# Expert step of a mixture-of-experts layer: rows turned behind the gather, down weights laid as 8 KB runs

## The reference

```python
gu = xb @ w_up[e] + b_up[e]                  # (rows, 1024) x (1024, 2048)
gate, up = gu[:, :D_EXPERT], gu[:, D_EXPERT:]
gate = jnp.minimum(gate, SWIGLU_LIMIT)
up = jnp.clip(up, -SWIGLU_LIMIT, SWIGLU_LIMIT)
act = (up + 1.0) * (gate * jax.nn.sigmoid(SWIGLU_ALPHA * gate))
return act @ w_down[e] + b_down[e]           # (rows, 1024) x (1024, 1024)
```

## Time and profile before

| | before |
|---|---|
| median of three runs | 1363.99 us |
| the profiled execution's own time | 1364.04 us |
| its span, first to last instruction | 1362.3 us |
| PE busy / DVE / ACT / POOL | 1196.0 / 584.2 / 255.3 / 494.5 us |
| DMA packets, bytes | 110953, 448.96 MB |
| HBM read | 447.00 MB |

### The profile page before, as it was taken

The page is one execution under the profiler, slowest core; times in us unless marked ns, Lnnn a source line. Parts: engine busy times, 40 slices in busy tenths (PEclk is TensorE's granted clock), DMA queues, the critical chain, the costliest instruction groups (busy, mean ns, idle before and its releaser), DMA issues.

```text
span 1362.3 us, 30127 instructions
## 1 busy us (share of the span) xinstructions
PE 1196.0 (88%) x11131; PEld 585.9 (43%) x11132; DVE 584.2 (43%) x1229; ACT 255.3 (19%) x497; POOL 494.5 (36%) x813
## 2 busy tenths in 40 slices
PE   5899999999999997797699779869799798699996
PEld 3677777775543343232233223323234233233333
DVE  0699971211353443433244424424244344244444
ACT  3001122200122221221122112111122121122222
POOL 0183120000141344455444544544445445444330
PEclk9898999999799999998899889989899899899998
DMA  8963333345489599999999999999999999999981
GB/s 255 317 196 108 111 119 124 99 153 220 174 358 382 197 397 418 418 418 417 419 417 416 416 419 418 418 418 418 416 416 417 417 418 414 418 418 409 398 345 59
DMA packets 110953, 448.96 MB, mean 330 GB/s; under 512 B 8526, under 2 KB 42894, under 8 KB 78107
## 3 DMA queue, kind: packets, MB, share of 16 engines
q1 hardware_dynamic: 110190, 446.57, 83.0%
q10 hardware_dynamic: 685, 1.17, 0.3%
q0 software_dynamic: 48, 0.85, 0.2%
HBM read 447.00 MB, written 2.42 MB: 330 GB/s over the span
## 4 chain that ended last, share of the span: by engine, by line
PE 60%; DMA 11%; POOL 8%; issue 8%; DVE 7%; SPq 5%; ACT 0%; DVEq 0%; POOLq 0%
PE banks L1290 21%; PE banks L1093 12%; PE banks L1300 12%; DMA ring<-in_w_down 10%; POOL ring L508 6%; DVE R L762 4%; PE banks L1021 3%; SPq L383 3%; PE banks L1075 3%; PE banks L1054 2%; PE banks L1205 2%; POOL big L477 1%; PE banks L1061 1%; POOL prod L499 1%; PE banks L1084 1%
## 5 line engine op out<-in xcount | busy, mean ns | idle before, releaser
L1290 PE MATMUL banks<-ring,hT 128*32 128x512 f32 x3328 | 441.5, 625 | 99.1 <-POOL ring L508 84.2
L508 POOL COPY ring<-big 128x512 f32<-128x512 f32 x248 | 142.2, 621 | 567.9 <-SPq L389 567.9
L508 POOL COPY ring<-R 128x512 f32<-128x512 f32 x496 | 287.1, 623 | 133.4 <-DMA R<-in_w_up 131.2
L309 DVE TENSOR_TENSOR xt<-xt,banks 128x1024 f32<-128x1024 f32 x106 | 128.8, 1215 | 432.6 <-PE banks L1075 432.6
L1300 PE MATMUL banks<-ring,hT 128*32 128x256 f32 x3328 | 229.8, 396 | 11.5 <-DMA ring<-in_w_down 10.0
L1093 PE MATMUL banks<-hT,ring 128*128 128x288 f32 x768 | 195.6, 417 | 7.9 <-ACT stage L535 6.0
L1290 PEld LDWEIGHTS banks<-ring,hT 128*32 128x32 f32 x3328 | 98.7, 113 | 236.2 <-POOL ring L508 106.5
L1300 PEld LDWEIGHTS banks<-ring,hT 128*32 128x32 f32 x3328 | 110.5, 115 | 196.9 <-issue 129.4
L1093 PEld LDWEIGHTS banks<-hT,ring 128*128 128x128 f32 x768 | 149.3, 196 | 50.6 <-ACT stage L535 6.4
L654 ACT COPY WT<-banks 128x256 f32<-128x256 f32 x52 | 19.4, 372 | 537.9 <-PE banks L1300 537.9
L762 DVE SCALAR_TENSOR_TENSOR R<-big,convw,R 128x256 f32<-128x256 f32 x240 | 99.7, 490 | 0.0
(11 more groups left out here) (225 smaller groups left out, 770.3 us busy)
## 6 DMA issues: line engine op xcount, KB each, us to landing
ring<-in_w_down SPq DMA_DIRECT2D x128, 1024.0 KB, 11.7
R<-in_w_up SPq DMA_DIRECT2D x124, 1024.0 KB, 18.2
ring<-in_w_up SPq DMA_DIRECT2D x70, 1024.0 KB, 9.4
big<-in_w_up SPq DMA_DIRECT2D x62, 1024.0 KB, 14.1
ring<-in_w_in SPq DMA_DIRECT2D x24, 1024.0 KB, 10.0
ring<-in_w_branch_b SPq DMA_DIRECT2D x4, 1024.0 KB, 4.9
ring<-in_w_branch_a SPq DMA_DIRECT2D x4, 1024.0 KB, 4.9
ring<-in_w_out SPq DMA_DIRECT2D x4, 1024.0 KB, 4.9
```

The lines of the kernel that those rows point to most:

```text
L309: nc.vector.tensor_tensor(dst, dst, rows, ALU.add).then_inc(y_added, 1)
L508: ins = nc.gpsimd.tensor_copy(ring[:, k, h * 512:(h + 1) * 512], parked[k][:, h * 512:(h + 1) * 512])
L1290: ins = mm(UP[g * BLK:(g + 1) * BLK, :], xT[:, k, :], ring[:, k, g * 512:(g + 1) * 512], start=k == 0, stop=k == UP_SLOTS - 1)
```

## The change

Three things change together. The down load puts rows 2p and 2p+1 of its 256 rows into partition p, one run of 8 KB; so that the activations meet the right weight rows, `turn_raw` and the turning of `b_up` take every second column of a block of 256 (a step of 8 bytes in SBUF) instead of 128 neighbouring ones. The sampled tokens' share goes to `DN[:, 256:512]` instead of `XB[:, 0:256]`; with that the wait for `rows_ready` in `combine_before` goes, and the first `down` step of a body (and of the tail) waits for DVE to have read it (`y_added` at `i * NT + 2`), since it lies in the bank that `down` writes. `turn_rows` moves from behind `combine_before` to right behind `turn_raw`.

```diff
@@ load_slot @@
                     src = a["w_down"][0, bass.ds(e, 1), j * 256:(j + 1) * 256, :].rearrange(
-                        "e (h p) n -> p (e h) n", p=P)
-                    dst = ring[:, k, :].rearrange("p (h n) -> p h n", h=2)
+                        "e (p h) n -> p (e h n)", p=P)
+                    dst = ring[:, k, :]
@@ add_before @@
-                add_output(dve, row_out[tt], tt) if tt < 2 else add_quarters(dve, XB[:, 0:256])
+                add_output(dve, row_out[tt], tt) if tt < 2 else add_quarters(dve, DN[:, 256:512])
@@ the turning of b_up @@
+                    pairs = bup_rows.rearrange("e (b p h) -> e b h p", h=2, p=P)
                     for f in range(2 * KC):
-                        ins = tr(bank[5][:, f * NE:(f + 1) * NE], bup_rows[:, f * P:(f + 1) * P])
+                        ins = tr(bank[5][:, f * NE:(f + 1) * NE], pairs[:, f // 2, f % 2])
@@ turn_raw, combine_before @@
+                pairs = raw.rearrange("t (b p h) -> t b h p", h=2, p=P)
                 for c in range(4):
-                    ins = tr(TB[:, c * P:(c + 1) * P], raw[:, c * P:(c + 1) * P])
+                    ins = tr(TB[:, c * P:(c + 1) * P], pairs[:, c // 2, c % 2])
                 ins.then_inc(raw_turned, 1)
 
-            def combine_before(i, rows):
-
-                pe.wait_ge(rows_ready, rows)
+            def combine_before(i):
+
                 pe.wait_ge(y_added, i * NT + 1)
                 combine(1, row_out[1])
-                combine_sample(XB[:, 0:256])
+                combine_sample(DN[:, 256:512])
@@ the body @@
                 turn_raw(i)
-                combine_before(i, i + 2)
                 turn_rows(i + 1)
+                combine_before(i)
                 turn_weights(i)
                 pe.wait_ge(xT_ready, i + 2)
                 for k in range(UP_SLOTS):
                     up(k, after)
                     if k == 1:
                         pe.wait_ge(act_ready, i + 1)
+                        pe.wait_ge(y_added, i * NT + 2)
                     if 1 <= k <= DOWN_SLOTS:
                         down(k - 1, here)
@@ the tail @@
-            combine_before(bodies, bodies + 1)
+            combine_before(bodies)
             turn_weights(bodies)
             pe.wait_ge(act_ready, bodies + 1)
+            pe.wait_ge(y_added, bodies * NT + 2)
```

## The result

The changed kernel takes 1351.08 us (median of 5 runs, 1348.94 to 1353.08), the kernel before in the same comparison 1359.66 us (5 runs, 1359.11 to 1364.49). The ratio is 0.9926 with a 95% interval of 0.9911 to 0.9941: 0.74% faster, 8.6 us between the medians and some 10 us by the ratio. The forecast was 0.69% and 1354.6 us. One run of the kernel before, in the comparison of c1_after, took 1550.63 us at a mean clock of 0.74 and is left out of every ratio and count.

The account below looks back on a forecast made before the run. PE was taken to bound 383 to 503 and 1209 to 1347 us, the weights' DMA queue the 706 us between. Terms -6.1 - 3.9 + 0.3 + 0.3 = -9.4 us from 1364.04 gave 1354.6 us, range 1350 to 1366 us.

Parts of the forecast that it names:

- the base: Whole kernel: the profiled 1364.04 us, within 0.05 us of the runs' median, from which 9.4 us were subtracted.
- Down load: Queue-bound stage, 503 to 1209 us: 8 KB runs save 0.28 us per expert, 22 experts, 6.1 us.
- Rival 1: Down loads: the rate does not hang on the run, the 6.1 us stay; 1360.7 us, chance 0.13.
- Rival 3: Down loads: half the rate difference belongs to the run, 3.1 us instead of 6.1; 1357.6 us, chance 0.10.
- The early turning: PE-bound stages: PE's wait for DVE's `take_x` goes, 0.30 us in 13 of 15 bodies, 3.9 us.
- a slowed one: A body where POOL copies beside DVE: nothing won, and the first down step's wait for L313 costs 0.3 us.
- the tail: After the last body: no `turn_rows` there, only the new wait for L313 is left, 0.3 us lost.
- Rival 2: 80 strided transposes cost PE: +11.2 us at one more load time each, +22.4 us at two; chance 0.13.
- Rival 4: Wait for L313 ahead of `down` binds everywhere: 3.9 us not won, 13 bodies lose 0.3 us; 1362.4 us, chance 0.04.
- The fixed cost of a packet: Down loads: by the skill's three cycles per packet 2.6 us over 22 experts; the windows' 2.8% rate difference was taken instead.

Follow-up runs that it names:

- c1_after: The changed kernel measured again with no edit: 1353.03 us, ratio 0.9923 against the kernel before.
- e5_2kb: Kernel with the early turning alone, its down slots reordered so that a run is 2 KB: 1373.45 us, ratio 1.0090 against the kernel before.
- e6_16kb: Changed kernel with down loads of 2 MiB in 16 KB runs, every fourth column turned, slots released in pairs: 1361.05 us, ratio 0.9998 against the kernel before.
- e2_turn: Changed kernel with the old 4 KB down load and old turning, leaving the early turning, other bank and its wait: ratio 0.9984 against the kernel before.
- e3_plain_turn: Changed kernel with up product and up bias turned from neighbouring columns, so the output is wrong: ratio 0.9917 against the kernel before.
- e7_keep: Changed kernel with the routing stage's filler matmuls 128 columns wide instead of 32: 1350.09 us, ratio 0.9922 against the kernel before.
- e9_shift_keep: Changed kernel with down steps one up step later, the tail's sampled-share addition between swish steps, and 128-column fillers: 1348.83 us, ratio 0.9902 against the kernel before.
- e8_before_keep: Kernel before with only the routing stage's fillers widened to 128 columns: 1357.50 us against 1363.57 us, ratio 0.9961.
- c2_after: The changed kernel measured once more with no edit, for direct comparison on the same chip: 1355.78 us, ratio 0.9944 against the kernel before.

## Why the prediction was right, and where it failed

**The step that failed is the base.** "Against the profiled execution's 1364.04 us ... that makes 1354.6 us. The median of the runs is 1363.99 us, the same within 0.05 us": three runs and one profile were taken for the level of the kernel before. Its times lie in two heaps: of 60 runs 27 took 1362.3 us or less (from 1358.46), 30 took 1363.5 us or more (up to 1366.26), and three lie between. The five of the comparison that counts had a median of 1359.66 us, 4.3 us under the base. From there 1354.6 us is only 5.1 us down, 0.37%, about half of the 0.74% measured, though the sum itself forecast 9.4 us. Over all 60 runs the median is 1363.25 us and over the 17 of the changed kernel without any edit 1353.08 us, 10.2 us apart, so which heap the few runs of a comparison fall into is luck in both directions. The profile had the long stretch at 1.2 GHz; c1_after has it too and took 1354.06 us, 0.5 us from the forecast. The trace of before showed the stretch (PEclk 0.50 from 360 to 372 us), and nothing of it stood in the working. Its two lengths in the traces differ by 3.5 us, and the mixing's end moves by up to 5 us from profile to profile (350.6 to 355.4 us at its last group of 16 matmuls): as much as half of the effect to be predicted.

**Down load, -6.1 us: right in cause, too small.** Middle stage 710.7 us on average over the six profiles with the new layout, the loads of the change and the down steps in their place (709.92, 710.66, 710.95, 710.97, 711.05, 710.41) against 717.9 us over three with the old (717.85, 718.17, 717.79): 7.3 us. Inside a down load 421 to 423 GB/s instead of 409.7. The landings of the loads say the same over the whole stage: a down load of 1 MiB lands 2.560 us behind the one before it with 4 KB runs and 2.485 us with 8 KB runs (medians, before and after), while the up loads, in 8 KB runs both times, land 2.49 us apart. That is 0.30 us for an expert, and the stage holds 24 of them (96 down loads are issued in it): 7.2 us. The term had 0.28 us and 22 experts; the factor was too careful, no gain was lost where the queue was thinner. Rival 1 is out: with the same run `w_down` lands as fast as `w_up`, and by e5_2kb and e6_16kb the rate goes with the run. Rival 3 is out as well: all of the difference belongs to the run.

**The early turning, -3.9 us in 13 of 15 bodies, +0.3 us in a slowed one, +0.3 us in the tail: -3.3 us.** Bodies at full speed went from 16.05 to 15.74 us, 0.31 us (0.30 forecast). By stages it is 3.1 us in e2_turn's profile (2.06 + 1.31 + 0.08 gained, 0.32 lost in the middle) and 2.2 us by the ratio. The working names two slowed bodies and counts the loss of one. Between the gathers of the two PE-bound stages there are 14 intervals in each profile; from before to after eleven are 0.25 to 0.34 us shorter, two stay (16.07 to 16.03 us, 16.05 to 16.08 us), and the first of the loop grows from 16.20 to 16.44 us. The body of 16.03 us is the one shown at 1237.98: PE starts its up steps 0.3 us earlier in it and gives 0.23 us back at the new wait, so such a body loses nothing against before, where 0.3 us of loss was forecast. The body of 16.08 us has the one wait for L747 that is left. In the tail the new wait is there as forecast, 1.23 to 1.56 us, and the stride adds 0.1 us beside it; together they cancel the last body's gain, so that the time from the last gather to the end stays at 35.55 us.

**Rival 2, the stride: out, but not by the test that was given.** The text said that a weight load of 200 ns or more means rival 2. The load is 202 ns, and e3_plain_turn shows that it costs nothing that the ratio can tell; the traces show 0.1 us in the tail. The duration of an overlapped instruction is no price; the distance between the starts of the matmuls is. The Trainium skill (SBUF — State Buffer, "Door 1: The DMA port swizzle") wants two accesses in a line of 16 bytes, by which the step of 8 bytes was to be free. The time of the body agrees with it, the load itself does not: it went from 140 to 202 ns, and a step of 16 bytes, with one access in a line, gave the same 202 ns.

**Rival 4: out.** From the first up matmul to the first down matmul it is 1.74 us in six of the eight last bodies of after and 1.98 and 1.99 us in the other two, of which one had 1.95 us before the change too. Beside them the wait binds in the first body of the loop (2.10 us, not in c1_after) and in the tail.

**The fixed cost of a packet.** The Trainium skill (DMA: Bandwidth & Descriptors, "Why small descriptors are slow (HBM only)") gives a fixed cost of three cycles; the rates say about 9 ns for each packet on its DMA engine. Three cycles at the 850 MHz of that page are 3.5 ns, an estimate, and the measured cost is 2.6 times that. The direction is the page's, the size is from the windows, and the choice for the windows was right.

## What to carry to other kernels

Where a queue is saturated, read its rate in windows that hold one kind of load, and price the run length by the difference; here doubling 4 KB runs gave 0.3 us of 10.24 us for each 4 MiB. The next doubling, bought with a release of slots in pairs, raised the rate inside the loads and lost the whole gain elsewhere. Before an effect of under 1% is set against a base, look into the profile for a stretch that can be long or short by chance (here the clock ahead of the loop), and say for which case the base stands. A few runs are no base where the times of a kernel lie in two heaps. A transfer that is the bound hides every saving on the engine behind it, so count bodies only in the stages that the engine bounds.

## What the runs showed of the hardware

- The time of a packet on its DMA engine, from the rates of full windows (bytes x 16 / rate): 2 KB 84.7 ns (387 GB/s), 4 KB 160 ns (409.7), 8 KB 311 ns (421.4), 16 KB 613 ns (427.5, mean of 429 and 426). Twice one less the next is 9.4, 9 and 9 ns: a constant for each packet from 2 to 16 KB. The median distance of the down loads' landings gives the same: 2.710, 2.560 and 2.485 us for 1 MiB and 4.897 us for 2 MiB.
- LDWEIGHTS of 128x128 float32 takes 140 ns from neighbouring columns, 202 ns at a step of two and 202 ns at a step of four. Behind two more transposes it is hidden (1.00 us for six in either case); four strided transposes alone take 0.75 instead of 0.65 us.
- PE's clock fell to 1.2 GHz between 356.7 and 359.4 us in every profile with the narrow fillers, after products mostly of 32 columns, with which PE was busy 4.00 of 4 us (354 to 358 us in after and c1_after), and near one idle time of 0.40 us. It stayed there for 6.8, 10.2 or 13.6 us. In e7_keep and e9_shift_keep, where the fillers among them were 128 columns wide, it stayed at 2.4 GHz; in e8_before_keep with the same fillers it fell for 3.4 us.
- The last item's 64 products took 3.66 us at 2.4 GHz and 5.35 us where the clock was at 1.2 GHz for 3.4 us of them (c2_after, e3_plain_turn).
